# Start offsets modulo 512 bytes of the buffers that TensorE reads

## The reference, cut to what matters

```python
def first_block(x, ...):
    x = _layer_norm(x, ln_emb_g, ln_emb_b)
    proj = x @ w_in[l]                        # 1024 x 3592
    ...                                       # attention and a gated recurrence
    mix = concatenate([o_a, o_r], -1) @ w_o[l]
    x = _layer_norm(DEEPNORM_ALPHA * x + mix, ln_mix_g[l], ln_mix_b[l])
    h = _causal_depthwise_conv(x @ w_up[l], conv_w[l], conv_b[l])   # 1024 x 5632
    a, u = jnp.split(h, 2, axis=-1)
    ffn = (jax.nn.gelu(a) * u) @ w_down[l]    # 2816 x 1024
    return _layer_norm(DEEPNORM_ALPHA * x + ffn, ln_ffn_g[l], ln_ffn_b[l])

def second_block(x, c, ctx, ...):
    # h = modulated rmsnorm(x); products with w_in (1024 x 5120); neighbourhood attention,
    # long convolutions as products with DFT tables, gated merge, then
    x = x + g2 * ((silu(h2 @ ffn_w1) * (h2 @ ffn_w3)) @ ffn_w2)     # 1024 x 2816, twice, and back
    return rmsnorm(x, final_g)
```

## Time and profile before

| | us |
|---|---|
| median of 3 runs | 1586.36 |
| lowest and highest | 1585.63, 1590.94 |
| span of the profiled execution, first to last instruction | 1583.9 |
| PE busy | 1534.6 |
| PE weight loads busy | 1296.2 |
| DVE busy | 1022.9 |
| ACT busy | 691.7 |
| POOL busy | 433.9 |

### The profile page before, as it was taken

The page is one execution under the profiler, slowest core; times in us unless marked ns, Lnnn a source line. Parts: engine busy times, 40 slices in busy tenths (PEclk is TensorE's granted clock), DMA queues, the critical chain, the costliest instruction groups (busy, mean ns, idle before and its releaser), DMA issues. The chain is left out here.

```text
span 1583.9 us, 21018 instructions
## 1 busy us (share of the span) xinstructions
PE 1534.6 (97%) x8432; PEld 1296.2 (82%) x8432; DVE 1022.9 (65%) x1547; ACT 691.7 (44%) x1020; POOL 433.9 (27%) x367
## 2 busy tenths in 40 slices
PE   5999998999999999999999999998999999999997
PEld 5778886778888888887988878886778999999886
DVE  7676457778677765668643544338855799985324
ACT  5644346745533344223623344443445544543222
POOL 0024315622411211000160022214442666650002
PEclk9999999999999999999999999999999999999999
DMA  7342112452344423665424322305362133324211
GB/s 306 107 146 94 60 58 90 150 216 101 122 163 144 183 80 120 232 247 199 145 106 132 115 97 90 124 33 174 140 231 84 54 109 113 107 102 156 97 63 54
DMA packets 50987, 203.61 MB, mean 129 GB/s; under 512 B 18528, under 2 KB 18784, under 8 KB 32138
## 3 DMA queue, kind: packets, MB, share of 16 engines
q1 hardware_dynamic: 37346, 172.04, 30.1%
q0 software_dynamic: 8576, 28.29, 4.9%
q10 hardware_dynamic: 4968, 1.94, 0.5%
HBM read 181.24 MB, written 21.00 MB: 128 GB/s over the span
## 5 line engine op out<-in xcount | busy, mean ns | idle before, releaser
L582 PE MATMUL ps<-xl,whi 128*128 128x512 f32 (+1 forms) x1136 | 395.1, 348 | 0.0
L1852 DVE TENSOR_TENSOR wlo<-raw,whi 128x2048 fp32r<-128x2048 f32 x89 | 221.7, 2491 | 144.2 <-ACT whi L1211 144.1
L1211 ACT ACTIVATE whi<-raw 128x512 fp32r<-128x512 f32 (+1 forms) x191 | 232.3, 1223 | 130.6 <-PE ps L583 87.7
L581 PE MATMUL ps<-xh,whi 128*128 128x256 f32 (+1 forms) x768 | 263.6, 343 | 6.2 <-DVE xl L1896 6.2
L583 PE MATMUL ps<-xh,wlo 128*128 128x256 f32 (+1 forms) x768 | 258.4, 337 | 0.0
L582 PEld LDWEIGHTS ps<-xl,whi 128*128 128x128 f32 x1136 | 215.2, 189 | 28.9
L581 PEld LDWEIGHTS ps<-xh,whi 128*128 128x128 f32 x768 | 145.4, 189 | 29.7 <-issue 15.7
L583 PEld LDWEIGHTS ps<-xh,wlo 128*128 128x128 f32 x768 | 144.8, 189 | 16.3
L581 PE MATMUL ps<-xhr,whi 128*128 128x512 f32 (+1 forms) x368 | 137.7, 374 | 2.3 <-DVE xl L1896 2.3
L583 PE MATMUL ps<-xhr,wlo 128*128 128x512 f32 (+1 forms) x368 | 139.4, 379 | 0.0
L2284 DVE SCALAR_TENSOR_TENSOR xr<-ps,pc,xr 128x511 f32<-128x511 f32 x88 | 65.4, 747 | 43.0 <-ACT xr L1211 41.5
(11 more groups left out here) (468 smaller groups left out, 3654.9 us busy)
## 6 DMA issues: line engine op xcount, KB each, us to landing
raw<-in_w_in SPq DMA_DIRECT2D x35, 1024.0 KB, 5.0
raw<-in_ffn_w SPq DMA_DIRECT2D x33, 1024.0 KB, 4.8
raw<-in_ada SPq DMA_DIRECT2D x24, 1024.0 KB, 4.8
raw<-in_w_up SPq DMA_DIRECT2D x22, 1024.0 KB, 4.8
raw<-in_w_down SPq DMA_DIRECT2D x11, 1024.0 KB, 5.3
xd<-X POOLq DMA_DIRECT2D x8, 512.0 KB, 6.0
td<-vr POOLq DMA_DIRECT2D x16, 256.0 KB, 3.5
raw<-td SPq DMA_DIRECT2D x4, 1024.0 KB, 4.7
```

The lines of the kernel that those rows point to most:

```text
L581: pe.e.matmul(o, lh, rh, start=start, stop=False)
L582: pe.e.matmul(o, lh, rl, start=False, stop=False)
L1211: m = ac.e.activation(dst, src, func, **more)
L1852: up(ve.e.tensor_tensor(lo, raw[conv_at[j] % 3][:, :], hi.bitcast(F32), ALU.subtract), "wlo")
```

## The change

It reorders the requests for small buffers, adds one that nobody reads or writes (`fill`, 160 bytes) and moves two (`onesf`, `msk`) into inner stacks, over places that are free at that time. No instruction is added, removed or moved on any engine; every instruction reads and writes the same names as before, at other addresses.

```diff
         X, Xr = twins("X", [P, 4, D], ctx)
         raw = [sb("raw", [P, 2048]) for _ in range(3)]
+        mod = sb("mod", [P, 64])
         whi = [sb("whi", [P, 2048], F32R) for _ in range(2)]
         wlo = [sb("wlo", [P, 2048], F32R) for _ in range(2)]
-        pc = sb("pc", [P, NPC])
-        ident = sb("ident", [P, P])
-        onesf = sb("onesf", [P, P])
         eps = sb("eps", [P, 2])
         cs = sb("cs", [P, 16])
+        sb("fill", [P, 40])
         bc, bc_r = twins("bc", [P, 2 * D], ctx)
         bcg, bcb = bc[:, 0:D], bc[:, D:2 * D]
-        mod = sb("mod", [P, 64])
+        ident = sb("ident", [P, P])
+        pc = sb("pc", [P, NPC])
         small = sb("small", [P, 288])
...
         el = sb("el", [P, 16], F32, xts)
+        onesf = sb("onesf", [P, P], F32, xts)
...
         bm = [sb("bm", [P, 512], F32, q2) for _ in range(3)]
-        msk = sb("msk", [P, 3, 32], F32, q2)
...
         rel = [rel0, sb("rel", [P, 8, 48], F32, f2)]
+        msk = sb("msk", [P, 3, 32], F32, f2)
```

## The result

| | before | changed |
|---|---|---|
| median, us | 1587.79 (4 runs) | 1566.18 (4 runs, 1564.40 to 1568.53) |
| ratio, 95% interval | | 0.9863 (0.9847 to 0.9879) |
| span of the profiled execution, us | 1583.9 | 1565.6 |

The change is 21.6 us faster, 1.4%. Measured again beside the experiments, the kernel before had medians of 1587.3 to 1587.8, and the changed one 1567.91. Two executions among the later ones were far slower than all others (3897 us of the kernel before, 3061 us of e4) and stand in no ratio.

The account below looks back on a forecast made before the run. TensorE, busy 97% of the span, was taken to bound the kernel through its matmul pitch; gains at 512 columns minus 0.4 us at 256 made 27.8 us less, 1586.4 to 1558.6 us, range 1552 to 1588.

Parts of the forecast that it names:

- D 256 is D 0: Operand starts 256 bytes apart (D, modulo 512) cost what equal starts do: 226.9 ns at 512 columns, 27.8 us less.
- Rival (a): Pattern is 512 bytes long, distance 256 acts like its neighbours: 233.3 ns at 512 columns, 5.2 us less; chance 0.30.
- (b): At distance 256 the streams never meet: 215.9 ns at 512 columns, about 100 us less in all; chance 0.10.
- (c): Distance 256 costs one step of 6.7 ns more than its neighbours: 240.0 ns at 512 columns, 26 us more; chance 0.10.
- Rival (d): Matmul pitch hangs on something that goes with the stage, offsets have no part: time stays at 1586.4 us; chance 0.10.
- the five 256-column pitches fall evenly modulo 256: Reason for a 256-byte period: ordered modulo 256, distances 0, 96, 128, 160, 224 give 120.0, 120.0, 118.6, 118.6, 118.4 ns.
- The doubt that went with it: In 256-column matmuls, all rows at 120.0 ns have the moving operand at 480, all below have it elsewhere.
- The picture of a load that meets the stream once or twice: Stationary load and moving stream slide past by some 512 bytes, meeting once if the pattern is 512 bytes, twice if 256.
- the period of 256 bytes: In TensorE's operand reads, the memory pattern repeats after 256 bytes, so distance 256 costs what distance 0 does.
- The sum: Over all matmuls: 12.8, 9.2, 5.4, 0.2 and 0.6 us less, 0.4 more; together 27.8 us less.
- The forecast's own: Range of the likeliest case alone, 1552 to 1566 us, for a pitch 1 to 2 ns beside that at distance 0.

Follow-up runs that it names:

- e4: Changed kernel with the shared weight buffers at 256 modulo 512, all else at 128 (operand distances 128 and 384): 1587.37 us, ratio 0.9991.
- e1: Changed kernel with `mod` behind the shared weight buffers, so `whi` and `wlo` lie at 128 like all else (distance 0 everywhere): 1565.96 us, ratio 0.9860.
- e2: Kernel before with `eps`, `cs` and `mod` ahead of the shared weight buffers, moving `whi` and `wlo` from 128 to 480: 1571.77 us, ratio 0.9898.
- e9: Changed kernel with the shared weight buffers at 288 modulo 512, all else at 128 (distances 160 and 352, as commonest before): 1589.65 us.
- e7: Changed kernel with `whi` at 128 modulo 512 like all else (distance 0) and `wlo` alone at 256 (distance 128): 1580.00 us.
- e3: Changed kernel with the shared weight buffers at 192 modulo 512, all else at 128 (distances 64 and 448): 1578.40 us, ratio 0.9937.
- e10: The changed kernel once more, unaltered, for comparison and a second profile: 1567.91 us, ratio 0.9869 to the kernel before.
- e5: Changed kernel with the shared weight buffers at 160 modulo 512, all else at 128 (distances 32 and 480): 1587.45 us.

## Why the prediction was right

**The bound** was read rightly: PE's pitch was all, and nothing that feeds it became late (0.7 us more for weight tiles).

**D 256 is D 0** was taken "narrowly", with a chance of 0.40. It holds exactly: 226.7 and 120.0 ns. Rival (a) named the same stretch and wanted 233.3; (b) wanted 216, (c) 240. Rival (d) falls with e1, e2 and e9: the two operands of a stream cost up to 7.6 ns more a matmul, 3%, by their distance alone. For TensorE's own two reads the rule of the Trainium skill (SBUF - State Buffer, Who interferes with whom), that they go through independent ports and that TensorE waits on nobody, therefore doesn't hold here.

**The reasons given for it** were weaker than the result. That the five 256-column pitches fall evenly modulo 256 was an accident of which five distances the kernel had: with 64 (113.3 or 117.8) and 192 put in, nothing falls evenly. The doubt that went with it, that 480 and not the distance made 120.0, is refuted by the changed kernel's own 120.0 with the moving operand at 128, and by e9. The picture of a load that meets the stream once or twice wasn't borne out by e7, and gives no two pitches for one distance, as e3 has. So the period of 256 bytes was there, but that the forecast took it rather than rival (a) was in part luck. Two smaller readings were off as well. The clock wasn't full throughout, since the page's tenths hide the stretch of 6.8 us. And rival (c) would have decided from 234.6 ns on and not 234.9 (5.2 us over 4152 matmuls are 1.25 ns); nothing hangs on it.

**The sum** said 27.8 us less; it was 21.6, and 18.3 in the profiled executions. Matching the float32r matmuls of both traces one by one gives where the 18.5 us between first and last went:

| steps | before to after, us | forecast |
|---|---|---|
| 512 columns, unbroken | -25.2 | -28.2 |
| 256 columns, unbroken | +0.3 | +0.4 |
| steps across a pause (waits, other instructions) | +3.1 | 0 |
| half-clock stretches | +3.2 | 0 |

The term that was mis-sized is the first: the forecast multiplied every matmul by the pitch of a long row. Of 4344 matmuls of 512 columns 220 are followed by a pause, and after a pause the row needs some nine steps to find its pitch: the first six steps mean 231.7, 233.4, 231.7, 228.4, 229.7 and 230.5 ns, and from the tenth on it is 226.7. Before, no such ramp is to be seen (233.5, 231.8, 233.6, 231.3, ...), since the settled pitch is no lower. So the unbroken steps fell by 6.1 ns on average and not by 6.6. By an estimate from these figures, half of the missing 3.0 us is the ramp and half the steps next to a pause, which were counted too. The second is the waits, which the prediction put at nothing: at the turning points DVE and ACT set the time, and a TensorE that comes earlier waits longer (all waits of PE together 40.4 us before, 43.0 after). The third is the half clock. Both kernels have 6.8 us of it before their last matmul, but near the start, where TensorE waits anyway, it cost nothing (the matching steps of the changed kernel, at full clock, differ by 0.1 us), and amid the matmuls it costs some 3 us. It is partly chance: of this same kernel a second profile (e10) had 25.3 us from the unbroken steps again, but 9 to 10 us more at half clock and 1 to 2 less in pauses, together 8.8 us, where 5 to 8 were expected. Three of its six stretches (the others, 3.4 us each, begin near 1075, 1085 and 1119 us):

```profile
17.10:23.80 6.70, 4.18 (x19) 4.21 (x20) 2.95 (x7) 5.58 (x8) 1.61 (x3) 0.50 1.01 353
273.10:276.30 3.20, 3.20 (x14) 2.72 (x13) 3.14 (x9) 2.24 (x7) 2.90 (x4) 0.50 0.09 33
368.70:375.30 6.60, 5.96 (x18) 5.07 (x19) 4.08 (x11) 5.17 (x11) 0.00 (x0) 0.50 0.01 4
```

Whether a faster TensorE meets more of them than the kernel before can't be told: of that one there is only one profile (6.8 us at half clock). The twelve others had 3.4 to 27.3 us, and among them the three kernels that are as slow as the one before (e5, e9, e4) had 6.8, 10.2 and 17.1 us.

**The range** of 1552 to 1588 held the time. The forecast's own, 1552 to 1566, missed it by 0.2 us, for the ramp, the waits and the clock.

## What to carry to other kernels

Where TensorE's pitch is the bound, look at the distance between the starts of its two operands modulo 256 bytes, which costs a few lines of padding: for moving operands of 512 columns of float32r put it at 0, for 256 columns at 64 or 192, and measure, since at 512 columns nothing of the gain is left 32 bytes beside the right place. Steps finer than 32 bytes weren't tried, nor other element types. A natural experiment is often in the trace already: the same instruction on operands at different distances, each over a long unbroken row. When turning a pitch into a time, count only the steps that aren't next to a pause, and expect the waits at turning points to take back a part.

## What the runs showed of the hardware that was not expected

- One distance can have two stable pitches (228.9 and 233.3 ns at D 64 with 512 columns, 113.3 and 117.8 at D 448 with 256), each kept over a hundred matmuls and more.
- 512 and 256 columns have different best distances: at D 0 the former are quickest (226.7) and the latter slowest (120.0).
- The quickest 256-column row, 113.3 ns, is 6.6 ns over the bare columns; the quickest of 512, 226.7, is 13.4 over. The 518 cycles (215.8 ns) that the Trainium skill gives as the gap of isolated matmuls of 512 columns (TensorE: Matmul & The Clock Gate, Back-to-back issue gap) were reached at no distance.
- After a pause a row at D 0 or 256 takes about nine matmuls to reach its pitch (231.7 ns at first, 226.7 from the tenth on).
- The granted clock falls to half for 3.4 or 6.8 us at a time, at a few places (near 17, 273, 370 and 397 us, and from one to three times between 1075 and 1135 us), in some executions and not in others. Of what sets it off the runs show little.
